# A sliding-window attention with 8 heads inside a three-layer fp32 model step: scores over valid blocks only, the band added by matmul, values divided as they leave PSUM, gates kept in SBUF

## The chip, the core and the metric

One NeuronCore of a Trainium2 chip runs one program. The metric is the device time of one execution in microseconds (us), the median of three runs. TensorE does the matmuls, ScalarE (ACT) and VectorE (DVE) evacuate and transform, GpSimd (POOL) helps, SyncE (SP) starts the weight transfers.

## The reference, cut

The program computes three layers on 512 tokens of width 1024: a first block (a mixer of a gated linear recurrence and a banded attention, a cross-attention to 256 memory tokens, a feed-forward part), and two layers more with five feed-forward parts in all, a latent attention and a gated convolution. The change is in the first block's mixer. Its banded attention has 8 query heads of 64 on 2 key heads; each block of 128 queries sees keys at most 128 away, and each head has a sink in the denominator:

```python
valid = (jnp.abs(qi - kj) <= WINDOW) & (kj >= 0) & (kj < S)
s = jnp.where(valid[None, :, None, None], s, -jnp.inf)
m = jnp.maximum(jnp.max(s, axis=-1, keepdims=True), sk)
p = jnp.exp(s - m)
p = p / (jnp.sum(p, axis=-1, keepdims=True) + jnp.exp(sk - m))
o = jnp.einsum('bnhgqk,bnkhd->bnqhgd', p.astype(v.dtype), vb)
...
merged = jax.nn.sigmoid(gate_r) * y_rec + jax.nn.sigmoid(gate_a) * y_att
return merged @ w_out
```

## The kernel before

Activations lie feature-major: 8 tiles of 128 features x 512 tokens. A weight chunk is 128 x 2048, loaded by SyncE to one of two `stage` slots, and split by ScalarE into a rounded `w_hi` (`split_hi`) and by VectorE into the rest `w_lo` (`split_lo`). A product of two fp32 numbers is three fp32r matmuls (`products`: hi x hi, hi x lo, lo x hi, lines 1744 to 1746); a chunk gives two tiles of 512 tokens, 48 matmuls. Matmuls on plain fp32 operands are recorded as two passes. The order on each engine is the order in which its block of the program is written; semaphores tie the engines. `acc_evac` counts evacuated tiles, `chunk_done` chunks, `lo_ready` split chunks. PSUM has 8 banks of 512 columns; projections rotate through banks 0 to 3.

The stretch of the change comes after the recurrence's twelve chunks ("gla"). First, chunk `kv_a`: tile k feature-major, tile v token-major in 96 matmuls of 128 columns. Then the rotary embedding of k and of four tiles of q: `swap` exchanges feature halves by a matmul with `perm1`, `rotate` on VectorE needs three operations. k stands in `k_pad` with zero blocks at both ends, so that every query block has 384 keys.

Attention runs in tiles j of two heads (p = 0, 1). `scores` (PE) writes 4 blocks x 384 columns to banks 0 to 3, for both heads the same ones; `maxima` (DVE) adds `band` into `w_s` in SBUF, which frees the banks, and takes the maxima; `exponentials` and `divided` (ACT) each pass over `w_s`; `turn` (PE) transposes the ten valid 128 x 128 pieces to banks 4 to 6; ACT rounds them to `wT_hi`, DVE computes `wT_lo`; `values` (PE) makes 12 matmuls into bank 7. A head's `turn` waits for `divided`. The first merge branch is put between the last two heads.

Merge: 8 branches of 24 matmuls, `BRANCHES` alternating the recurrent side (0) and the attention side (1) of output pairs j. Each is multiplied by its gate on DVE. Gate pairs of j = 0, 1 are in `h` (whose residual is read back from DRAM later), those of j = 2, 3 are written to DRAM (`spill`) during gla and read back as `late` and `late_att`. The memory tokens (`mem_raw`) are fetched after the attention; GpSimd sums their squares; a matmul with ones (line 2027) after branch 4 spreads the sum; DVE normalizes four of the eight tiles inside the loop over branches after number 5 and four after it. Then comes the chunk phase `mix_out`.

The same program has a second attention, in the latent layer (8 heads, causal). There the band's counterpart is added by a matmul with the identity, exponentials read PSUM, the transposed probabilities stay fp32, and outputs come token-major, divided on evacuation and transposed back.

## Time and profile before

| | us |
|---|---|
| median of 3 runs | 2855.84 (2854.48 to 2856.95) |
| the profiled execution, its own time | 2857.13 |
| its span, first to last instruction | 2855.3 |
| TensorE busy in the span | 2797.6 (98%) |
| VectorE / ScalarE / GpSimd busy | 1452.4 / 1031.5 / 532.6 |
| stretch from the end of gla to `mix_out` | 298.3 to 457.3 |
| mean granted TensorE clock | 0.990 |

Times in rows are us from the span's start; a row of the timeline has start, duration, engine, line, operation, output<-inputs, partitions x elements, count, and in brackets the idle time before it and what ended that.
### The profile page before, as it was taken

The numbers are of one execution on the slowest core, as the hardware profiler recorded it, in microseconds if no ns is written. First come the engines' busy times: TensorE is split into PE (matmuls) and PEld (weight loads), VectorE is DVE, ScalarE is ACT, GpSimd is POOL, SyncE is SP. The second block draws the span as 40 slices with busy tenths as digits, with TensorE's granted clock in tenths as the row PEclk, the third lists the DMA queues.
The fourth block names the chain that finished last, engine by engine and source line by source line (L and its number), as shares of the span: only waits on it lengthen the run. The fifth ranks groups of instructions, "written<-read, shape, count | busy, mean of one in ns | idle before, by whom it ended". The sixth has DMA issues, their size and how long they took to land.

```text
span 2855.3 us, 33812 instructions
## 1 busy us (share of the span) xinstructions
PE 2797.6 (98%) x12830; PEld 2310.8 (81%) x12830; DVE 1452.4 (51%) x1378; ACT 1031.5 (36%) x1136; POOL 532.6 (19%) x374
## 2 busy tenths in 40 slices
PE   8999888999999999999999999999999999999999
PEld 6978677987888888888868888888888888888887
DVE  5777756547655344443475544334444355644432
ACT  3333553344443234332244343323433222244421
POOL 1124013104001221023230310022100221410100
PEclk9999889999999999999999999999999999999999
DMA  4222113412223332323310222233222332222232
GB/s 161 76 73 96 49 66 104 146 54 103 98 93 103 103 103 88 103 90 106 122 56 31 103 90 101 100 106 103 89 103 88 104 103 102 94 98 95 96 103 88
DMA packets 39818, 270.72 MB, mean 95 GB/s; under 512 B 4416, under 2 KB 4928, under 8 KB 8000
## 3 DMA queue, kind: packets, MB, share of 16 engines
q1 hardware_dynamic: 37152, 259.01, 26.5%
q10 hardware_dynamic: 2592, 10.65, 1.0%
q8 instruction: 55, 0.90, 0.1%
q14 instruction: 19, 0.16, 0.0%
HBM read 265.45 MB, written 4.19 MB: 94 GB/s over the span
## 4 chain that ended last, share of the span: by engine, by line
PE 95%; DVE 2%; ACT 2%; POOL 1%; DMA 1%; issue 1%; ACTq 0%; DVEq 0%; POOLq 0%; SPq 0%
PE ps L1744 30%; PE ps L1746 30%; PE ps L1745 30%; PE ps L1900 1%; PE ps L2248 1%; PE ps L1922 0%; PE ps L2222 0%; PE ps L2146 0%; PE ps L1973 0%; ACT w_s L613 0%; POOL sq L1660 0%; DVE w_lo L898 0%; DMA mem_raw<-in_mem 0%; ACT w_s L622 0%; PE ps L1784 0%
## 5 line engine op out<-in xcount | busy, mean ns | idle before, releaser
L438 ACT ACTIVATE w_hi<-stage 128x2048 fp32r<-128x2048 f32 x241 | 462.1, 1918 | 1378.3 <-PE ps L1746 1376.3
L1744 PE MATMUL ps<-x_hi,w_hi 128*128 128x512 f32 x2392 | 940.7, 393 | 12.4 <-DVE w_lo L973 12.4
L1745 PE MATMUL ps<-x_lo,w_hi 128*128 128x512 f32 x2392 | 931.9, 390 | 0.0
L1746 PE MATMUL ps<-x_hi,w_lo 128*128 128x512 f32 x2392 | 931.8, 390 | 0.0
L898 DVE TENSOR_TENSOR w_lo<-stage,w_hi 128x2048 fp32r<-128x2048 f32 x241 | 605.4, 2512 | 402.0 <-ACT w_hi L438 402.0
L1744 PEld LDWEIGHTS ps<-x_hi,w_hi 128*128 128x128 f32 x2392 | 449.8, 188 | 108.3 <-DVE x_lo L980 12.4
L1745 PEld LDWEIGHTS ps<-x_lo,w_hi 128*128 128x128 f32 x2392 | 449.9, 188 | 95.0 <-issue 3.1
L1746 PEld LDWEIGHTS ps<-x_hi,w_lo 128*128 128x128 f32 x2392 | 449.7, 188 | 94.2
L1744 PE MATMUL ps<-f_hi,w_hi 128*128 128x512 f32 x880 | 342.7, 389 | 0.0
L1745 PE MATMUL ps<-f_lo,w_hi 128*128 128x512 f32 x880 | 342.3, 389 | 0.0
L1746 PE MATMUL ps<-f_hi,w_lo 128*128 128x512 f32 x880 | 342.3, 389 | 0.0
L1614 POOL TENSOR_TENSOR up_b<-up_b,gate_b 128x512 f32<-128x512 f32 x110 | 118.1, 1095 | 1050.9 <-DVE up_b L961 1034.7
L961 DVE TENSOR_TENSOR up_b<-ps,rstd 128x512 f32<-128x512 f32 x110 | 71.0, 687 | 299.2 <-PE ps L1746 299.1
L1745 PEld LDWEIGHTS ps<-f_lo,w_hi 128*128 128x128 f32 x880 | 165.2, 188 | 34.7 <-issue 0.2
L1744 PEld LDWEIGHTS ps<-f_hi,w_hi 128*128 128x128 f32 x880 | 165.2, 188 | 34.6 <-issue 0.2
L1746 PEld LDWEIGHTS ps<-f_hi,w_lo 128*128 128x128 f32 x880 | 165.2, 188 | 34.1
L944 DVE TENSOR_TENSOR gate_b<-ps,rstd 128x512 f32<-128x512 f32 x110 | 71.0, 688 | 230.2 <-PE ps L1746 229.1
L1590 POOL TENSOR_TENSOR sq<-h 128x512 f32 x64 | 78.6, 1228 | 503.6 <-DVE h L923 497.5
L1592 POOL TENSOR_TENSOR ssum<-ssum,sq 128x512 f32<-128x512 f32 x64 | 141.9, 2218 | 5.0
L923 DVE SCALAR_TENSOR_TENSOR h<-ps,h 128x512 f32 (+1 forms) x72 | 46.4, 686 | 141.0 <-PE ps L1746 136.8
L929 DVE SCALAR_TENSOR_TENSOR x_lo<-h,par,x_hi x64 | 104.2, 1666 | 0.0
L485 ACT ACTIVATE f_hi<-up_b 128x512 f32 x110 | 69.6, 633 | 26.9 <-POOL up_b L1614 22.7
(398 smaller groups left out, 2787.6 us busy)
## 6 DMA issues: line engine op xcount, KB each, us to landing
stage<-in_stream SPq DMA_DIRECT2D x242, 1024.0 KB, 4.9
h<-in_x SPq DMA_DIRECT2D x4, 512.0 KB, 7.2
spill<-late ACTq DMA_DIRECT2D x4, 512.0 KB, 2.6
h<-in_x ACTq DMA_DIRECT2D x2, 1024.0 KB, 5.2
out_x<-h SPq DMA_DIRECT2D x8, 256.0 KB, 6.0
stage<-in_stream SPq DMA_DIRECT2D x4, 256.0 KB, 8.1
late<-spill ACTq DMA_DIRECT2D x1, 1024.0 KB, 5.0
late_att<-spill ACTq DMA_DIRECT2D x1, 1024.0 KB, 7.1
```

Of the source, the lines that this page charges most:

```text
L438: act.activation(w_hi[slot][:, :], stage[slot][:, :], ACT.Copy).then_inc(hi_ready, 1)
L485: act.activation(row(f_hi, it * 2 + e), up_b[:, e, :], ACT.Copy).then_inc(f_hi_ready, 1)
L898: dve.tensor_tensor(w_lo[slot][:, :], stage[slot][:, :], w_hi[slot][:, :].bitcast(F32), ALU.subtract).then_inc(lo_ready, 1)
L929: dve.scalar_tensor_tensor(row(x_lo, it * 4 + m), row(h, it * 4 + m), pc(gain, it * 4 + m), row(x_hi, it * 4 + m).bitcast(F32), ALU.mult, ...
L944: dve.tensor_tensor(gate_b[:, e, 1:1 + S], ps[:, (t0 + e) % 4, :], rstd[:, :], ALU.mult).then_inc(acc_evac, 1)
L961: dve.tensor_tensor(up_b[:, e, :], ps[:, (t0 + 2 + e) % 4, :], rstd[:, :], ALU.mult).then_inc(acc_evac, 1)
L1590: pool.tensor_tensor(sq[:, :], row(h, m), row(h, m), ALU.mult).then_inc(sq_ready, 1)
L1592: pool.tensor_tensor(ssum[:, :], ssum[:, :], sq[:, :], ALU.add).then_inc(ss_ready, 1)
L1614: pool.tensor_tensor(up_b[:, e, :], up_b[:, e, :], gate_b[:, e, 1:1 + S], ALU.mult).then_inc(prod_ready, 1)
L1744: pe.matmul(out_ap, wh, xh, start=first, stop=False)
L1745: pe.matmul(out_ap, wh, xl, start=False, stop=False)
L1746: return pe.matmul(out_ap, wl, xh, start=False, stop=last)
```

## The change

Storage and banks. The two heads of a tile get score banks of their own (2, 3, 4 and 0, 1, 5); the turned pieces go back to the same banks. `w_s`, `w_pT` and `mem_raw` take the place of `x_hi` and `x_lo`, which are free once `kv_a` is done. The gates have room in SBUF, `late` and `late_att`, and the DRAM spill is gone.

```diff
+        k_f = place("k_f", TMP, [P, S])
+        k_hi, k_lo = place("k_hi", hid(20), [P, S], F32R), place("k_lo", hid(21), [P, S], F32R)
+        w_s = [place(f"w_s{e}", XH_AT + 3 * e * TILE, [P, 3, S]) for e in range(2)]
+        w_pT = [place(f"w_pT{e}", XH_AT + (6 + 3 * e) * TILE, [P, 3, S]) for e in range(2)]
+        w_o = [place(f"w_o{e}", TMP + (1 + e) * TILE, [P, BLK, P]) for e in range(2)]
...
+        v_f, va = place("v_f", hid(24), [P, S]), place("va", hid(14), [P, BLK, P])
+        wa_const = place("wa_const", hid(12), [P, 4 * P])
+        band, perm1 = wa_const[:, 0:384], wa_const[:, 384:512]
+        wa_const_r = place("wa_const_r", hid(13), [P, 4 * P], F32R)
+        band_r, eye_r = wa_const_r[:, 0:384], wa_const_r[:, 384:512]
...
-        mem_raw = place("mem_raw", hid(16), [P, KT, MEM])
+        mem_raw = place("mem_raw", XH_AT + 12 * TILE, [P, KT, MEM])
...
+        WINDOW_BANKS = [[2, 3, 4], [0, 1, 5]]
+        WINDOW_AT = {1: (0, 0), 2: (1, 0), 0: (2, 0), 3: (2, 2 * P)}
+        WINDOW_OF = TURNED_OF
+        WINDOW_ORDER = [[1], [2], [0, 3]]
+        ROTATED = ["q0", "q1", "q2", "k", "q3"]
+        SWAP_BANK = [5, 6, 7, 5, 6]
```

ScalarE. All gates pass the sigmoid before the last gla chunk's split. Exponentials read PSUM; the division is gone; the third bank's turned piece is a plain copy. `mem_raw` is fetched when `kv_a` is done. Later, the memory's square root and rounding come after all branches.

```diff
-                    spilled_out(3)
+                    act.wait_ge(acc_evac, t + 10)
+                    act.activation(h[:, :, :], h[:, :, :], ACT.Sigmoid).then_inc(gate_sig, 1)
+                    act.activation(late[:, :, :], late[:, :, :], ACT.Sigmoid)
+                    act.activation(late_att[:, :, :], late_att[:, :, :], ACT.Sigmoid).then_inc(gate_sig, 1)
...
-                    act.activation(w_s[p][:, n, :], w_s[p][:, n, :], ACT.Exp, bias=small[:, 4 * p + n:4 * p + n + 1],
-                                   accum_out=small[:, 8 + 4 * p + n:9 + 4 * p + n])
+                    b, c = WINDOW_AT[n]
+                    w = len(WINDOW_OF[n]) * P
+                    act.activation(w_s[p][:, b, c:c + w], ps[:, WINDOW_BANKS[p][b], c:c + w], ACT.Exp,
+                                   bias=small[:, 4 * p + n:4 * p + n + 1], accum_out=small[:, 8 + 4 * p + n:9 + 4 * p + n])
...
-            act.wait_ge(spilled, 64)
-            act.dma_start(late[:, :, :], spill[:, 0:4, :]).then_inc(gates_back, 16)
-            act.dma_start(late_att[:, :, :], spill[:, 4:8, :]).then_inc(gates_back, 16)
+            q_round(1)
+            act.wait_ge(rot_step, 3 * (ROTATED.index("k") + 1))
+            act.activation(k_hi[:, :], k_f[:, :], ACT.Copy).then_inc(k_hi_ready, 1)
+            act.wait_ge(chunk_done, C0["kv_a"] + 1)
             act.dma_start(mem_raw[:, :, :], mem_in).then_inc(mem_landed, 16)
+            exponentials(0)
...
+            exponentials(1)
+            turned(0)
+            q_round(2)
+            for v in range(1, WIN_HEADS):
+                turned(v)
+                if v + 1 < WIN_HEADS:
+                    exponentials(v + 1)
+                if v == 2:
+                    q_round(3)
+                if v == 4:
+                    split_hi((C0["kv_a"] + 2, 0))
+                if v % 2 == 0:
+                    out_hi(v // 2 - 1)
...
-                if j == 2:
-                    act.wait_ge(mem_stat, 1)
-                    act.activation(mem_r, ps[:, 5, 0:MEM], ACT.Sqrt, bias=pc("eps", 0), scale=1.0 / D).then_inc(mem_std, 1)
-                    mem_rounded(0, 4)
...
-            mem_rounded(4, KT)
+            act.wait_ge(mem_stat, 1)
+            act.activation(mem_r, ps[:, 5, 0:MEM], ACT.Sqrt, bias=pc("eps", 0), scale=1.0 / D).then_inc(mem_std, 1)
+            mem_rounded(0, KT)
```

VectorE. Maxima read PSUM per bank. The turned copy replaces the remainder `wT_lo`; `out_divided` multiplies by the reciprocal of the denominator. The rotations of q0 and q1 stand before the evacuation of k. All of the memory's normalization comes after the branches.

```diff
+                for bank, blocks in enumerate(WINDOW_ORDER):
+                    dve.wait_ge(wa_scores, 3 * v + bank + 1)
+                    for n in blocks:
+                        b, c = WINDOW_AT[n]
+                        w = len(WINDOW_OF[n]) * P
+                        ins = dve.tensor_reduce(mx[:, n:n + 1], ps[:, WINDOW_BANKS[p][b], c:c + w], AX.X, ALU.max)
+                ins.then_inc(wa_max, 1)
...
+                dve.tensor_copy(w_pT[p][:, 0:2, 0:384], ps[:, b0:b0 + 2, 0:384]).then_inc(wa_pT, 1)
...
+                dve.tensor_tensor(w_o[j % 2][:, :, half], ps[:, 6, :].rearrange("p (a n) -> p a n", a=BLK)[:, :, half],
+                                  free(small[:, 24 + 4 * p:28 + 4 * p], 0, [[1, BLK], [0, WIN_D]]), ALU.mult).then_inc(wa_ot, 1)
...
+            rotate(0, qa[:, 0, :])
+            rotate(1, qa[:, 1, :])
+            dve.wait_ge(kv_done, 1)
+            dve.scalar_tensor_tensor(k_f[:, :], ps[:, t0 % 4, :], WIN_D ** -0.5, rstd[:, :], ALU.mult, ALU.mult).then_inc(acc_evac, 1)
+            rotate(2, qa[:, 2, :])
+            rotate(3, k_f[:, :])
+            dve.wait_ge(k_hi_ready, 1)
+            dve.tensor_tensor(k_lo[:, :], k_f[:, :], k_hi[:, :].bitcast(F32), ALU.subtract).then_inc(k_ready, 1)
+            rotate(4, qa[:, 3, :])
...
+            maxima(0)
+            maxima(1)
+            for v in range(WIN_HEADS):
+                denominators(v)
+                turned(v)
+                if v:
+                    out_divided(v - 1)
+                if v == 5:
+                    split_lo((C0["kv_a"] + 2, 0))
+                if v and v % 2 == 0:
+                    out_lo(v // 2 - 1)
+                if v + 2 < WIN_HEADS:
+                    maxima(v + 2)
...
-                if i == 5:
-                    dve.wait_ge(mem_std, 1)
-                    dve.reciprocal(mem_r, mem_r).then_inc(mem_std, 1)
-                    dve.wait_ge(mem_std, 2)
-                    mem_normed(0)
-                    for k in range(4):
-                        mem_normed(k + 1)
-                        mem_rest(k)
-            for k in range(4, KT):
```

TensorE. The swaps are spread around the two halves of `kv_a`, and v is made feature-major and transposed by four matmuls. A head's scores take only the valid blocks (256, 384, 384, 256 columns) and add the band by a matmul with `eye_r`. Values are 10 fp32 matmuls of 64 columns. `back` transposes two heads' output. Branch 0 and 1 are spread around the last heads.

```diff
+            def swap(i, src):
+                pe.wait_ge(const_landed, 16)
+                if i >= 3:
+                    pe.wait_ge(rot_step, 3 * (i - 3) + 1)
+                pe.matmul(ps[:, SWAP_BANK[i], :], perm1, src, start=True, stop=True).then_inc(perm_done, 1)
+            def kv_tile(m, done):
+                for k in range(KT):
+                    mm = products(ps[:, (t + m) % 4, :], w_at(c, k * PAIR + m * P, P), (x_hi[:, k, :], x_lo[:, k, :]), k == 0, k == KT - 1)
+                mm.then_inc(done, 1)
+            pe.wait_ge(acc_evac, T0["gla"] + 12)
+            pe.wait_ge(ls_norm, 16)
+            swap(0, qa[:, 0, :])
+            swap(1, qa[:, 1, :])
             begin(c, t, 2)
-            for k in range(KT):
-                products(ps[:, t % 4, :], w_at(c, k * PAIR, P), (x_hi[:, k, :], x_lo[:, k, :]), k == 0, k == KT - 1)
-            for b in range(BLK):
-                for k in range(KT):
-                    mm = products(ps[:, (t + 1) % 4, b * P:(b + 1) * P], (x_hi[:, k, b * P:(b + 1) * P], x_lo[:, k, b * P:(b + 1) * P]),
-                                  w_at(c, k * PAIR + P, P), k == 0, k == KT - 1)
-            mm.then_inc(chunk_done, 1)
-            def swap(i, tile, src):
-                pe.wait_ge(acc_evac, tile + 1)
-                pe.wait_ge(const_landed, 32)
-                if i >= 4:
-                    pe.wait_ge(rot_step, 3 * (i - 4) + 1)
-                pe.matmul(ps[:, 4 + i % 4, :], perm1[:, :], src, start=True, stop=True).then_inc(perm_done, 1)
-            swap(0, T0["kv_a"], k_pad[:, P:P + S])
-            for i in range(WIN_TILES):
-                swap(1 + i, T0["gla"] + 12 * (i // 2) + 10 + i % 2, qa[:, i, :])
-            pe.wait_ge(acc_evac, T0["merge"])
-            pe.wait_ge(k_ready, 1)
-            def scores(j, p, first=False):
+            kv_tile(0, kv_done)
+            pe.wait_ge(acc_evac, t)
+            swap(2, qa[:, 2, :])
+            pe.wait_ge(acc_evac, t + 1)
+            swap(3, k_f[:, :])
+            swap(4, qa[:, 3, :])
+            kv_tile(1, chunk_done)
...
+                for blocks in WINDOW_ORDER:
+                    for n in blocks:
+                        b, at = WINDOW_AT[n]
+                        k0, w = WINDOW_OF[n][0] * P, len(WINDOW_OF[n]) * P
+                        out_ap = ps[:, WINDOW_BANKS[p][b], at:at + w]
+                        products(out_ap, (q_hi[j % 2][half, n * P:(n + 1) * P], q_lo[j % 2][half, n * P:(n + 1) * P]),
+                                 (k_hi[half, k0:k0 + w], k_lo[half, k0:k0 + w]), True, False)
+                        m0 = k0 - (n - 1) * P
+                        mm = pe.matmul(out_ap, eye_r, band_r[:, m0:m0 + w], start=False, stop=True)
+                    mm.then_inc(wa_scores, 1)
...
+                        mm = pe.matmul(ps[:, 6, n * P + WIN_D * p:n * P + WIN_D * (p + 1)], w_pT[p][:, at_bank, at:at + P], va[:, b, half],
+                                       start=(b == WINDOW_OF[n][0]), stop=(b == WINDOW_OF[n][-1]))
...
+            for v in range(WIN_HEADS):
+                turn(v)
+                if v:
+                    values(v - 1)
+                if v == 6:
+                    pe.wait_ge(wa_pT, v + 1)
+                    pe.wait_ge(wa_pT_act, v + 1)
+                    branch(0, range(3))
+                if v and v % 2 == 0:
+                    back(v // 2 - 1)
+                if v + 2 < WIN_HEADS:
+                    scores(v + 2)
+            branch(0, range(3, 4))
+            values(WIN_HEADS - 1)
+            branch(1, range(1))
+            back(3)
+            branch(1, range(1, 4))
...
-                if i == 4:
+                if i == 2:
```

On GpSimd the remainder `q_lo` goes to two buffers; the two memsets of `k_pad` are gone.

The order of instructions shows the moves. TensorE before, from the end of `kv_a` over the swaps (`perm_106`) to the first scores:

```order
L1746 MATMUL ps<-w_hi_54,x_lo 128x128
L1949 MATMUL ps<-k_pad,perm_106 128x512 [waits const_landed,acc_evac]
L1949 MATMUL ps<-qa,perm_106 128x512 [waits const_landed,acc_evac] x3
L1949 MATMUL ps<-qa,perm_106 128x512 [waits rot_step,const_landed,acc_evac]
L1744 MATMUL ps<-k_hi,q_hi 128x384 [waits wa_q,k_ready,acc_evac]
L1745 MATMUL ps<-k_lo,q_hi 128x384
```

TensorE after the change, between the k half (its last matmul first) and the v half of `kv_a` (the permutation is now part of `wa_const`):

```order
L1740 MATMUL ps<-x_hi,w_lo_56 128x512
L1935 MATMUL ps<-qa,wa_const 128x512 [waits const_landed,acc_evac]
L1935 MATMUL ps<-k_f,wa_const 128x512 [waits rot_step,const_landed,acc_evac]
L1935 MATMUL ps<-qa,wa_const 128x512 [waits rot_step,const_landed]
L1738 MATMUL ps<-x_hi,w_hi_54 128x512
L1739 MATMUL ps<-x_lo,w_hi_54 128x512
```

Three swaps moved from behind the chunk to between its halves; two more stand ahead of the k half.

TensorE before, inside the loop over tiles: a head's transposes and the next tile's scores, with their waits:

```order
L1973 MATMUL ps<-const_64,w_s_97 128x128 [waits wa_p]
L1973 MATMUL ps<-const_64,w_s_97 128x128 x9
L1961 REGISTER_ALU [waits wa_q]
L1744 MATMUL ps<-k_hi,q_hi 128x384 [waits wa_s]
L1745 MATMUL ps<-k_lo,q_hi 128x384
```

TensorE after, for head 2: transposes, values of head 1, the transposition back of heads 0 and 1, scores of head 4:

```order
L1991 MATMUL ps<-const_64,w_s_96 128x128 [waits wa_exp]
L1991 MATMUL ps<-const_64,w_s_96 128x128 x9
L2008 MATMUL ps<-va,w_pT_99 128x64 [waits wa_ot,wa_pT_act,wa_pT]
L2008 MATMUL ps<-va,w_pT_99 128x64 x9
L2020 MATMUL ps<-const_64,w_o_100 128x128 [waits va_ready,wa_ot]
L2020 MATMUL ps<-const_64,w_o_100 128x128 x3
L1738 MATMUL ps<-k_hi,q_hi_102 128x384 [waits wa_pT_act,wa_pT,wa_q]
```

The transposes wait for the exponentials and no longer for a division, and the values behind them are those of the head before.

VectorE before, in the merge after branch 5, where the memory's normalization begins:

```order
L898 TENSOR_TENSOR w_lo_57<-stage_53,w_hi_55 128x2048 [waits hi_ready]
L1262 TENSOR_TENSOR late_att<-late_att,late 128x512 [waits acc_evac] x2
L1265 TENSOR_TENSOR mrg_lo<-late_att,mrg_hi 128x512 [waits mrg_hi_ready] x2
L1268 RECIPROCAL rope_c<-rope_c 128x256 [waits mem_std]
L1242 SCALAR_TENSOR_TENSOR rope_s<-mem_raw,par,rope_c 128x256 [waits mem_std]
```

VectorE after, from the evacuation of branch 6 to the same normalization:

```order
L1262 TENSOR_TENSOR late<-late,ps 128x512 [waits gate_sig,branch_done]
L1262 TENSOR_TENSOR late<-late,ps 128x512
L1262 TENSOR_TENSOR late_att<-late_att,ps 128x512 [waits gate_sig,chunk_done]
L1262 TENSOR_TENSOR late_att<-late_att,ps 128x512
L893 TENSOR_TENSOR w_lo_56<-stage_52,w_hi_54 128x2048 [waits hi_ready]
L1267 TENSOR_TENSOR late_att<-late_att,late 128x512 [waits acc_evac] x2
L1270 TENSOR_TENSOR mrg_lo<-late_att,mrg_hi 128x512 [waits mrg_hi_ready] x2
L1272 RECIPROCAL rope_c<-rope_c 128x256 [waits mem_std]
```

The normalization moved behind the evacuations of branches 6 and 7.

## Rows read from the trace of the kernel before

**Rows 1.** The page, chain that ended last, share of the span by engine.
```profile
PE 95%; DVE 2%; ACT 2%; POOL 1%; DMA 1%; issue 1%; ACTq 0%; DVEq 0%; POOLq 0%; SPq 0%
```
**Rows 2.** TensorE's waits, 280 to 480: us in total, times, longest.
```profile
PE ps L1973 <- ACT w_s L622: 9.3, 5, 4.3
...
PE ps L1744 <- issue: 4.2, 1, 4.2
```
**Rows 3.** Busy time by stage; columns: length, PE, PEld, DVE, ACT, POOL, clock, DMA, GB/s.
```profile
298.30:303.50 5.20, 5.20 (x24) 4.30 (x24) 5.17 (x7) 5.10 (x5) 0.00 (x0) 1.00 0.00 0
...
314.40:336.60 22.20, 13.01 (x34) 8.18 (x34) 19.18 (x28) 10.57 (x22) 1.26 (x1) 0.67 0.00 1
336.60:405.20 68.60, 58.10 (x272) 51.05 (x273) 45.84 (x58) 49.06 (x117) 3.80 (x3) 0.78 0.04 16
405.20:457.30 52.10, 40.96 (x172) 33.08 (x171) 33.69 (x41) 20.30 (x20) 16.72 (x16) 0.91 0.46 162
```
**Rows 4.** TensorE's timeline around two waits, then busy time of two stretches.
```profile
354.13 1.31 PE L1973 MATMUL ps<-const,w_s 128*128 128x128 f32 x10 [1.61 <-ACT w_s L622]
356.94 0.68 PE L1744 MATMUL ps<-k_hi,q_hi 64*128 64x384 f32 x1 [1.50 <-POOL q_lo L1651]
...
457.30:461.70 4.40, 4.38 (x10) 3.50 (x11) 4.40 (x5) 0.45 (x1) 0.00 (x0) 0.50 0.02 4
...
356.90:366.60 9.70, 9.66 (x34) 8.90 (x34) 6.23 (x8) 5.17 (x14) 0.00 (x0) 0.50 0.00 0
```
**Rows 5.** TensorE's timeline: two score matmuls, two swaps of q.
```profile
367.44 0.33 PE L1745 MATMUL ps<-k_lo,q_hi 64*128 64x384 f32 x1
367.62 0.33 PE L1746 MATMUL ps<-k_hi,q_lo 64*128 64x384 f32 x1
...
319.54 1.88 PE L1949 MATMUL ps<-qa,perm 128*128 128x512 f32 x4
```
**Rows 6.** The second attention: TensorE's timeline, then busy time of four heads.
```profile
1508.78 1.10 PE L2222 MATMUL ps<-k_h,q_h 128*128 128x512 f32 x2 [1.80 <-ACT l_pT L837]
...
1511.41 1.26 PE L2234 MATMUL ps<-const,l_p 128*128 128x128 f32 x10
1512.51 2.34 PE L2248 MATMUL ps<-v_mla,l_pT 128*128 128x64 f32 x20
1514.69 0.65 PE L2222 MATMUL ps<-k_h,q_h 128*128 128x512 f32 x1
...
1521.25 0.66 PE L2258 MATMUL ps<-const,o_t 128*128 128x128 f32 x4 [0.52 <-DVE o_t L1500]
...
1517.30:1543.10 25.80, 24.73 (x178) 21.28 (x177) 19.31 (x44) 16.44 (x42) 0.00 (x0) 1.00 0.12 42
```
**Rows 7.** Timeline of VectorE and ScalarE; one group of the lines.
```profile
298.48 0.69 DVE L1153 TENSOR_TENSOR TA<-TA,g_silu 128x512 f32<-128x512 f32 x1
...
302.54 1.29 DVE L1160 TENSOR_TENSOR rec_lo<-TA,rec_hi 128x512 fp32r<-128x512 f32 x2
...
1523.18 1.86 DVE L1477 TENSOR_REDUCE small<-ps 128x1 f32<-128x512 f32 x4
...
298.37 1.92 ACT L438 ACTIVATE w_hi<-stage 128x2048 fp32r<-128x2048 f32 x1 [8.94 <-PE ps L1746]
...
301.35 1.28 ACT L596 ACT_TABLE_LOAD   x1
302.64 3.62 ACT L596 ACTIVATE h<-h 128x4096 f32<-128x4096 f32 x1
...
L613 ACT ACTIVATE w_s<-w_s,small 128x384 f32<-128x384 f32 x28 | 16.8, 610 | 0.0
```
**Rows 8.** Timeline of GpSimd, TensorE and VectorE in the merge.
```profile
416.82 0.61 POOL L1657 TENSOR_TENSOR ssum<-mem_raw 128x256 f32<-128x256 f32 x1 [40.83 <-DMA mem_raw<-in_mem]
...
434.17 1.22 PE L2027 MATMUL ps<-ssum,const 128*128 128x256 f32 x2 [6.96 <-POOL ssum L1662]
...
455.94 1.28 DVE L1257 TENSOR_TENSOR late<-late,ps 128x512 f32<-128x512 f32 x2
```

306 lines of the change are left out of this document (126 added, 180 removed).

## The prediction

> **What bounds the kernel now.** I read the chain of work that ended last first: 95% of it is TensorE [rows 1], so a change is worth what it takes out of TensorE's own time line, as work, as a wait or as a slow clock. Then TensorE's waits in the stretch that the change rewrites: 9.3 us for the divided probabilities, 4.2 in front of mix_out [rows 2], and 7.0 for GpSimd's sum of squares [rows 8]. Then the busy time by stage [rows 3]. From the end of the gla chunks (298.3) to the start of mix_out (457.3) it is 159 us: 5.2 for the k half of kv_a, 10.9 for its v half, 22.2 for rotation and first scores (TensorE busy 13.0, granted clock 0.67), 68.6 for the eight heads with the first 24 recurrent matmuls between them (busy 58.1, clock 0.78), 52.1 for the other seven branches (busy 41.0, clock 0.91). A wait here costs twice: after 1.61 us of waiting, ten transposes and 1.50 us more of waiting, the clock fell to the 1.2 GHz level and stayed for 9.7 us of dense work [rows 4].
>
> **Up to the first transposes** (298.3 to 336.6, 38.3 us). Prices at full clock: 24 matmuls of 512 columns 5.4 (the k half has 24 in a window of 5.2, the last one running on [rows 3]), so 0.227 each; a 384-wide one 0.175 from start to start; a swap, which is two passes, 0.9, from four passes in 1.88 [rows 5]. The v half becomes 24 matmuls of 512 columns in place of 96 of 128: 5.4 for the 10.9 between 303.5 and 314.4 [rows 3]. The five swaps stay, but two now run before the k half and three between the halves, so VectorE's rotations (three operations of the kind of which two take 1.29 [rows 7], about 2.1 with their handovers) run beside TensorE and not after it. New order: TensorE, done with gla at 298.3, waits 0.9 for the last norm product, which VectorE finishes at 299.2 [rows 7]; two swaps 1.8; k half 5.4; swap 0.9; wait; two swaps 1.8; v half 5.4. The wait is new: VectorE is busy to 303.8 [rows 7], then does two rotations (4.3) and the evacuation of k (0.7), so k is there at 308.8 and TensorE waits 1.3. That is 17.5, to 315.8. Behind each rotation's wait for its swap only the next rotation and the evacuations are queued on VectorE; the last rotation ends at 316.6, the evacuation of v at 317.3.
>
> Scores of one head: before 12 matmuls of 384. After, only valid blocks: six products of 384 and six of 256, and the band as two of 384 and two of 256; at 0.175, and 0.12 for 256 by proportion, 2.36. So two heads and four transposes of v take 5.2 (to 321.0). The first head's maxima (four reductions, 1.86 [rows 7]) wait for the evacuation of v, end at 319.5, its exponentials (four at 0.61 and a small one, 2.7) at 322.3. TensorE waits 1.3. Total: 24.1 for 38.3, a gain of 14.2. Bounds: 9 (the wait for k doubled, and the clock at half for the swaps as before) to 16 (both waits gone).
>
> **The eight heads** (336.6 to 405.2, 68.6 us). The second attention in this same kernel is already built in the new way, and its rows are the nearest: ten transposes 1.10 (1511.41 to 1512.51), 20 value matmuls of 64 columns 2.18 (1512.51 to 1514.69), four transposes back 0.66 with their drain, so 0.5, after a wait of 0.52; four heads took 25.8 us, 6.45 each, with TensorE busy 24.7 and clock 1.00 [rows 6]. New: 8 x (1.10 + 2.18) = 26.2; six scores 14.2; three transposes back 1.5; the first recurrent branch, 24 x 0.227 = 5.4; together 47.3. Waits: 0.5 before each of the three transposes back, 1.6; one for the first turned copy, which on ScalarE stands behind the copy of v and the second head's exponentials: these end at 325.5, the copy at 326.1, TensorE was free at 323.4, so 2.7 (the like wait in the second attention is 1.80 [rows 6]); and one around the fifth head, where the split of a merge chunk (w_hi, 1.9) goes ahead of an output's rounding on ScalarE, and VectorE's remainder, maxima and next copy queue behind it: 1.2, and 0.3 in front of the branch. Total 53.1 for 68.6, a gain of 15.5. Removed work that was hidden: VectorE's two passes over 1536 columns a head, ScalarE's four divisions. ScalarE needs about 3.7 a head (exponentials 2.7, a turned copy 0.6, its share of roundings) and VectorE 4.1 (maxima 2.1, the copy of 768 columns 1.0, the division 0.4, small ones), both under TensorE's 6.2. Bounds: 6.45 a head and the same branch and first waits give 61, a gain of 8; no fifth-head wait gives 17.
>
> **The merge** (405.2 to 457.3). Seven branches at 5.4 are 38.1 before and after. What goes: the wait of 7.0 for the sums [rows 8], since mem_raw is now fetched at the end of kv_a and GpSimd begins the sums once q_lo of the last tile is done (about 337), 17 us of work from its start at 416.8 to the matmul at 434.2 [rows 8], with some 25 us of room; the slow clock after it, 2.0 (52.1 less 38.1, 7.0, 4.2 and 0.7 for the sums' own matmul, rounded); the wait of 4.2, which is VectorE emptying branch 6 only at 455.94 because the memory's normalization stood ahead of it [rows 8]; and the slow start of mix_out, 10 matmuls in 4.4 us at clock 0.50 [rows 4], 2.1. What comes: a transposition back, 0.5. Gain 14.8. What is late next: the memory's normalization, about 10 us on VectorE, now stands between the merge and the first mix_out evacuation, so the split for mix_out's third chunk ends at about +22.4 us where TensorE wants it at +21.8: 0.7 lost, bounds 0 and 5.
>
> **The gates on chip.** No wait of TensorE names the spill [rows 2], so its removal alone gives nothing. The sigmoids (3.62 for h's 4096 columns, so about 1.9 for each late one's 2048, and a table load of 1.28) move into ScalarE's idle time of 8.94 ahead of the split at 298.37 [rows 7]: 8.7 of 8.94, at nothing; if that cover fell short, the split behind it and the recurrent rounding would be late by the shortfall, under 1 us.
>
> **The clock.** Between the first heads TensorE will wait 1.3, transpose for 1.1, and wait 2.7. Before, 1.61 and 1.50 around the same transposes were followed by 9.7 us at clock 0.50 [rows 4]; in the second attention a wait of 1.80 was not followed by one, since the two passes behind it took 1.10, the full rate [rows 6]. Mine is worse than both, so I count one slow spell of 5 to 10 us, which costs half of itself, as all of it is TensorE's: 3. Bounds 0 and 9 (two such spells).
>
> **The sum.** 14.2 + 15.5 + 14.8 - 0.7 - 3 = 40.8. Against the profiled run's own 2857.1 (span 2855.3 and 1.8 around it) that is 2816.3; that run stands 1.3 above the median of 2855.84, so 2815.0.
>
> **Rivals.**
> (a) No slow spell: waits as costed, clock at 1.00 throughout. 3 us more gain: 2812. For it: the second attention's clock [rows 6]. Against: the slow 9.7 us behind the wait at 356.94 [rows 4]. The Trainium skill, "TensorE: Matmul & The Clock Gate", section "HAM oscillation", ties the fall to one long idle stretch of the engine; none of the waits here is long, so by that rule this rival is the forecast and the time 2812. The trace before the change does not follow it: there the fall came between two short waits.
> (b) The clock falls again and again, as before the change. TensorE keeps waits of 0.5 every other head, and its score matmuls still use 64 rows. Clock 0.78 over the 53 us of the heads would cost 10 to 12 more than (a) has: 2823 to 2828. Against: TensorE's idle time in the heads' stretch falls from 10.5 us to 5.8, most of it at the start. The same page, section "A second HAM failure mode", tells of a clock that goes up and down where the engine idles briefly between groups of matmuls; by it the time would be this rival's, and the stretch before the change at 0.78 agrees.
> (c) The handoffs set the pace: reductions, exponentials, copies and small operations beside GpSimd's sums stretch each head to 8 us and over. 8 x 1.8 = 14 more: 2829 to 2835. Against: the second attention has the same chain at 6.45.
> (d) Slower than before. One mechanism: TensorE's clock stays at the 1.2 GHz level from the first waits at 307 on. Each 1 us of full-rate work then costs 1 us more, so it decides from 44 us of such work on, 88 us of slow running; the stretch to mix_out holds about 100 of it, and slow throughout it would give 2912. For it: the clock was 0.67 and 0.78 over the 90 us from 314.4 to 405.2 [rows 3]. Against: it was 0.91 and not 0.5 in the dense matmuls that follow.
> (e) The change does not do what it says, the waits moving elsewhere with no gain. The order of instructions shows fewer and denser matmuls, and the 7.0 and 4.2 have their causes removed in the order; I give it what "same" has.
>
> **Chances.** Forecast (2813 to 2821) 0.45, (a) and better (2806 to 2813) 0.23, (b) 0.18, (c) 0.09, (d) 0.02, (e) 0.03. The forecast alone is 2815. The range that leaves out two in ten goes from 2807 to 2828. A measurement of this kernel tells about 0.2% (5.7 us) from no change: faster 0.95, same 0.03, slower 0.02.
>
> **What would show it.** In the changed profile: kv_a's v half in about 5.4 us; TensorE waiting about 1.3 for k_f; the second scores ending near 321, the first transposes at about 322; the last value matmuls ending near 375; no wait for GpSimd's sums and none of 4 us before mix_out, which starts near 414; a granted clock of 1.00 but for one spell after 326. It is wrong if a head takes over 7 us with TensorE idle in it (a handoff I placed under cover), if the clock in the heads' stretch is under 0.85, or if mix_out's third chunk waits over 2 us.

## The result, and the profile after

The changed kernel takes 2830.5 us, the median of 20 runs, against 2856.66 for the kernel before, also 20 runs: ratio 0.9925, 95% interval 0.9908 to 0.9942, a gain of 26 us. Forecast were 2815.0 and a range of 2807 to 2828. It is faster, by two thirds of what was forecast. (Of the changed kernel's 28 executions, these and the 8 of section 9, seven took 2841 to 2859 at a mean clock of 0.985 to 0.992, which widens the interval of the ratio without moving the median; of the 26 executions of the kernels with k over 128 rows in sections 2, 4, 8 and 9 none took more than 2815.) The profiled execution has a span of 2827.8, 27.5 shorter than the one before, and its mean granted clock is 0.996.

The chain of work that ended last, by engine, answers to [rows 1]:

```profile
PE 97%; DVE 2%; ACT 1%; DMA 0%; issue 0%; POOL 0%; DVEq 0%; SPq 0%; POOLq 0%; ACTq 0%
```

TensorE's waits between 298 and 480 (us in total, times, longest) answer to [rows 2]. All of them are here:

```profile
PE ps L1738 <- ACT w_pT L628: 1.9, 1, 1.9
PE ps L1935 <- DVE k_f L1219: 1.9, 1, 1.9
PE ps L2020 <- DVE w_o L1207: 1.0, 2, 0.5
PE ps L1935 <- issue: 1.0, 1, 1.0
```

5.8 us in place of 30.9. The 9.3 for the probabilities and the 4.2 in front of mix_out are gone, and so is the 7.0 for the sums. Busy time by stage, with the columns of [rows 3]: kv_a and rotation, scores to the last values, the merge, the first ten weights or so of mix_out:

```profile
298.30:316.00 17.70, 15.03 (x56) 10.49 (x57) 16.60 (x22) 5.32 (x8) 3.06 (x2) 1.00 0.18 60
316.00:393.10 77.10, 74.13 (x413) 60.20 (x411) 34.98 (x79) 28.93 (x88) 12.48 (x17) 0.87 0.08 28
393.10:432.20 39.10, 39.10 (x176) 32.39 (x176) 24.12 (x31) 10.06 (x10) 0.52 (x1) 1.00 0.37 135
432.20:436.60 4.40, 4.40 (x21) 3.65 (x20) 3.47 (x3) 1.92 (x1) 0.00 (x0) 1.00 0.01 2
```

The merge is solid: 39.1 us, all busy, at full clock, and mix_out starts at full clock with 21 matmuls in 4.4 us, where [rows 4] has ten. What is long is the second row: 77.1 us in which TensorE is busy for 74.1. The forecast had 59.6 for it, 7.1 of them waits, and 3 more for a spell of slow clock, which it counted apart. So TensorE is not waiting for a handoff; its own work costs more than I priced it. TensorE's timeline shows which. This is one head's scores at full clock, the first and the third of its four blocks, then the first transposes (start, duration with drain; cost is the distance from start to start):

```profile
340.30 0.44 PE L1738 MATMUL ps<-k_hi,q_hi 64*128 64x384 f32 x1
340.59 0.34 PE L1739 MATMUL ps<-k_lo,q_hi 64*128 64x384 f32 x1
340.76 0.33 PE L1740 MATMUL ps<-k_hi,q_lo 64*128 64x384 f32 x1
341.02 0.44 PE L1979 MATMUL ps<-wa_const_r 128*128 128x384 f32 x1
341.39 0.44 PE L1738 MATMUL ps<-k_hi,q_hi 64*128 64x384 f32 x1
...
342.48 0.38 PE L1738 MATMUL ps<-k_hi,q_hi 64*128 64x256 f32 x1
...
343.34 0.38 PE L1738 MATMUL ps<-k_hi,q_hi 64*128 64x256 f32 x1
...
344.11 1.14 PE L1991 MATMUL ps<-const,w_s 128*128 128x128 f32 x9
```

Between two products the distance is 0.17, the price I used. From the last product to the band matmul (L1979) it is 0.26, from the band matmul to the next product 0.37, and from that product to the second 0.29. A block of 384 columns takes 1.09 (340.30 to 341.39) where 4 x 0.175 = 0.70 was priced, one of 256 takes 0.86 where 0.48 was, a head 3.81 (340.30 to 344.11) where 2.36 was. The shape column tells what changes at just these places: `64*128` for the products, `128*128` for the band matmul. The weight loads (PEld) of the same stretch:

```profile
340.59 0.18 PEld L1740 LDWEIGHTS ps<-k_hi,q_lo 64*128 64x128 f32 x1
341.02 0.19 PEld L1979 LDWEIGHTS ps<-wa_const_r 128*128 128x128 f32 x1 [0.25 <-issue]
341.39 0.18 PEld L1738 LDWEIGHTS ps<-k_hi,q_hi 64*128 64x128 f32 x1 [0.18 <-issue]
341.50 0.19 PEld L1739 LDWEIGHTS ps<-k_lo,q_hi 64*128 64x128 f32 x1
```

A load between matmuls of one row count starts ahead of its matmul, beside the one that runs (340.59 for the matmul at 340.76). Where the row count changes, load and matmul start together (341.02, 341.39), and the loader has sat idle. Every head whose scores ran at full clock throughout takes 3.80 or 3.81, whichever 64 rows its products use.

The clock is the second thing. It is 0.87 in the stretch, with spells at 1.2 GHz from 324.8 to 338.5, from 352.0 to 355.3 and from 369.2 to 372.4. The first begins at the transposes that follow the second head's scores. The other two begin in the last matmuls of a head's scores, here the second:

```profile
352.04 0.31 PE L1740 MATMUL ps<-k_hi,q_lo 64*128 64x256 f32 x1
352.27 0.58 PE L1979 MATMUL ps<-wa_const_r 128*128 128x256 f32 x1
```

A band matmul of 256 columns takes 0.38 at full clock. None of the three has a wait directly ahead of it.

### The profile page after: what moved, and what is told of

Read it like the earlier page. It is cut to its first block, busy times and chain, and to the rows that moved or that the text cites. A ratio compares the mean times of both kernels' runs of the same rounds, so it can differ in the third digit from the quotient of the medians.

```text
span 2827.8 us, 33738 instructions
## 1 busy us (share of the span) xinstructions
PE 2794.9 (99%) x12874; PEld 2304.4 (81%) x12874; DVE 1429.2 (51%) x1387; ACT 1002.0 (35%) x1090; POOL 525.7 (19%) x372
## 4 chain that ended last, share of the span: by engine, by line
PE 97%; DVE 2%; ACT 1%; DMA 0%; issue 0%; POOL 0%; DVEq 0%; SPq 0%; POOLq 0%; ACTq 0%
PE ps L1738 30%; PE ps L1740 30%; PE ps L1739 30%; PE ps L1894 1%; PE ps L2008 1%; PE ps L2287 1%; PE ps L1916 1%; PE ps L2261 0%; PE ps L1979 0%; PE ps L2185 0%; PE ps L1991 0%; DVE w_lo L893 0%; DMA stage<-in_stream 0%; PE ps L1778 0%; DVE KK L1139 0%; PE ps L2273 0%
```

## The experiments

Two questions: what makes a head's scores dear, and what the clock does with them. Then, whether the terms for the merge were right. `products` has other line numbers (1752 to 1754) in kernels with k over 128 rows.

### 1. The band matmul over 64 rows

```
-  mm = pe.matmul(out_ap, eye_r, band_r[:, m0:m0 + w], start=False, stop=True)
+  mm = pe.matmul(out_ap, eye_r[half, :], band_r[half, m0:m0 + w], start=False, stop=True)
```

> The band's matmul is taken over 64 of its 128 rows (the half of the rows that the head's products use), so half of the band is not added; everything else is as in the changed kernel. Its profile shows one head's scores taking 3.81 us at full clock (340.30 to 344.11) where 2.36 was forecast: a block of three products (64 rows) and one band matmul (128 rows) takes 1.09 for 384 columns and 0.86 for 256, and the next weight load stands idle before each change of rows. Theory S (the change between 64-row and 128-row matmuls costs about 0.39 a block): all matmuls of the scores now have 64 rows, a head takes 2.36 to 2.5, eight heads save 10 to 12, time 2819 to 2821, and the low clock spells stay. Rival B (the band matmul is itself dear, through its operand or as fourth in an accumulation): a head stays at 3.8 and the time at 2830. Rival C (what is lost is mainly the clock, and only incidentally the switch): a head's scores get shorter, but the clock's slow spells grow and the time gains under 5.

Measured: 2816.78 (2815.66 to 2824.47), ratio 0.9862 (0.9845 to 0.9878). TensorE's timeline, with product, product, band, product, then the transposes of v behind the head:

```profile
316.58 0.33 PE L1739 MATMUL ps<-k_lo,q_hi 64*128 64x384 f32 x1
316.75 0.34 PE L1740 MATMUL ps<-k_hi,q_lo 64*128 64x384 f32 x1
316.93 0.34 PE L1979 MATMUL ps<-wa_const_r 64*128 64x384 f32 x1
317.11 0.34 PE L1738 MATMUL ps<-k_hi,q_hi 64*128 64x384 f32 x1
...
318.85 0.66 PE L2041 MATMUL ps<-const,v_f 128*128 128x128 f32 x4
```

The same number of matmuls with the same columns, and every distance is 0.17 to 0.18: a head takes 2.55 (316.30 to 318.85), and what it has over 2.36 lies at its edges, where its neighbours have 128 rows. The band matmul is not dear in itself, nor is it dear as the fourth in a sum: rival B has fallen. The gain of 13.7 is above the 10 to 12 of theory S; rival C expected under 5. In the profiled execution (the one at 2824.47) the low clock did not only stay: one spell of 27 us, from 327.8 to 355, takes the place of the three, and the gain there is only 5.2. The other three took 2815.7 to 2817.2. TensorE's clock is the last figure but two:

```profile
324.00:340.00 16.00, 13.91 (x62) 13.60 (x62) 5.54 (x12) 5.28 (x19) 1.28 (x1) 0.62 0.00 1
340.00:375.00 35.00, 33.96 (x213) 32.16 (x212) 18.67 (x43) 15.38 (x45) 11.22 (x16) 0.78 0.02 4
```

Inside a head's scores this kernel has no change of rows, only at their edges, so the low clock does not need the changes inside.

### 2. k over 128 rows

```
-  k_hi, k_lo = place("k_hi", hid(20), [P, S], F32R), place("k_lo", hid(21), [P, S], F32R)
+  k_hi = [place("k_hi0", hid(20), [P, S], F32R), place("k_hi1", hid(22), [P, S], F32R)]
+  k_lo = [place("k_lo0", hid(21), [P, S], F32R), place("k_lo1", hid(25), [P, S], F32R)]
...
-  products(out_ap, (q_hi[j % 2][half, n * P:(n + 1) * P], q_lo[j % 2][half, n * P:(n + 1) * P]),
-           (k_hi[half, k0:k0 + w], k_lo[half, k0:k0 + w]), True, False)
+  products(out_ap, (q_hi[j % 2][:, n * P:(n + 1) * P], q_lo[j % 2][:, n * P:(n + 1) * P]),
+           (k_hi[p][:, k0:k0 + w], k_lo[p][:, k0:k0 + w]), True, False)
```

> The computation is complete. k is kept twice, once with its lower and once with its upper 64 rows zero, so that each product runs over 128 rows with both heads' q as weights; GpSimd writes the four zero halves ahead of its first q_lo, ScalarE and VectorE write each half of k with an instruction of its own (two more instructions, under 1 us, which TensorE's v half covers by about 1). Theory S: all matmuls of the scores have 128 rows, a head takes 2.36 to 2.5 in place of 3.81, 10 to 12 less: 2819 to 2821 if the clock does as in the changed kernel. Theory L (the clock falls because 64-row matmuls make up most of the scores): the spells at 324.8 to 338.5, 352 to 355 and 369.6 to 372.3, which cost some 8 us, go as well: 2811 to 2814, granted clock above 0.98 from 316 to 393. Rival B (band matmul dear): 2830, head 3.8. Rival W (the clock falls because of the waits): scores shorter but the spells after 324.8 stay or grow.

Measured: 2812.25 (2811.81 to 2812.88), ratio 0.9847 (0.9831 to 0.9864), 18 us below the changed kernel; once more on another chip (section 9) 2814.61 beside 2830.10, 15.5 below. One head, from its first product to the transposes of v, and the stage from first scores to last values:

```profile
317.09 0.33 PE L1752 MATMUL ps<-k_hi,q_hi 128*128 128x384 f32 x1
317.26 0.34 PE L1753 MATMUL ps<-k_lo,q_hi 128*128 128x384 f32 x1
317.44 0.34 PE L1754 MATMUL ps<-k_hi,q_lo 128*128 128x384 f32 x1
317.62 0.35 PE L1994 MATMUL ps<-wa_const_r 128*128 128x384 f32 x1
317.80 0.34 PE L1752 MATMUL ps<-k_hi,q_hi 128*128 128x384 f32 x1
...
319.45 0.60 PE L2056 MATMUL ps<-const,v_f 128*128 128x128 f32 x4
...
317.10:376.10 59.00, 55.23 (x410) 53.44 (x409) 33.58 (x77) 29.13 (x88) 12.52 (x17) 0.97 0.11 36
```

317.09 to 319.45 is 2.36, the forecast's price to the hundredth (later heads take some 0.08 more, at the step from the fp32 matmuls ahead of them to their first product, 333.59 to 336.02). The stage takes 59.0 where the forecast had 59.6, and mix_out starts at 415.0 where the forecast's terms give 414.9, both without its slow spell of 3. That they come so close is in part luck: 3.3 less of waiting stands against a slow spell worth 1.7 and small terms. Zeros in half of the rows cost nothing: over 64 rows and over 128 a product of 384 columns takes 0.17 to 0.18 from start to start, so the 64 rows that were left out had been no saving. The clock shows one spell of 3.4 us behind the wait of 2.1 for the first turned copy, one of the same length during the rotations, and 1.00 from 330 on. Theory S holds. For theory L the time is inside its 2811 to 2814, and the stage's clock, expected above 0.98, is 0.97 because of that one spell.

### 3. The band matmuls grouped

```
+  for n in (1, 2, 0):
+      band_of(n, True)
   for blocks in WINDOW_ORDER:
       for n in blocks:
...
-          products(..., True, False)
-          mm = pe.matmul(out_ap, eye_r, band_r[:, m0:m0 + w], start=False, stop=True)
+          mm = products(..., n == 3, n != 3)
+          if n == 3:
+              mm = band_of(n, False)
```

> The computation is complete, and products keep 64 rows. The band matmuls of the first three blocks open their sums ahead of all products, the fourth's closes it behind them (two open sums may not stand in one bank), so a head changes between 128 and 64 rows once forth and once back, where the changed kernel does so four times. Theory S: three of four round trips of 0.39 go, 1.2 a head, 9 in all: 2821 to 2822, a head's scores 2.6 to 2.8. Rival B (the band matmul is dear in itself): a head stays at 3.8, 2830. Rival C (clock): the spells grow, under 5 gained.

Measured: 2821.03 (2819.64 to 2823.39), ratio 0.9881 (0.9864 to 0.9897): 9.5 less than the changed kernel, the expected 9. Here the price of one round trip can be read by itself, since a head has one:

```profile
317.23 0.62 PE L1974 MATMUL ps<-wa_const_r 128*128 128x384 f32 x3
317.78 0.44 PE L1738 MATMUL ps<-k_hi,q_hi 64*128 64x384 f32 x1
318.06 0.33 PE L1739 MATMUL ps<-k_lo,q_hi 64*128 64x384 f32 x1
...
319.73 0.39 PE L1974 MATMUL ps<-wa_const_r 128*128 128x256 f32 x1
319.95 0.60 PE L2048 MATMUL ps<-const,v_f 128*128 128x128 f32 x4
```

The head takes 2.72 (317.23 to 319.95), 0.36 over 2.36. The changed kernel has four round trips and takes 3.81, which is 2.36 + 4 x 0.36. Its blocks taken singly say much the same: 1.09 less 0.70 is 0.39, 0.86 less 0.48 is 0.38. (The head's 3.81 does not hold the first step from 128 rows to 64: it lies ahead of 340.30, and the four transposes of v in front of such a head take 0.53, in the kernel of 2 they take 0.36.) Two kernels, one price, 0.36 to 0.39.

### 4. Both together

```
+  for n in (1, 2, 0):
+      band_of(n, True)
...
+          mm = products(out_ap, (q_hi[j % 2][:, n * P:(n + 1) * P], q_lo[j % 2][:, n * P:(n + 1) * P]),
+                        (k_hi[p][:, k0:k0 + w], k_lo[p][:, k0:k0 + w]), n == 3, n != 3)
```

> The computation is complete: both edits together, k over 128 rows and the band matmuls ahead of the products. Theory S: no change of rows is left to save, so it equals the kernel with k over 128 rows alone within 1 us. Rival B' (part of the price is the band matmul following products into the same sum, not the change of rows): grouping gains again, 3 to 9 us below the kernel with 128 rows alone. It is also the candidate for the best version, with 2811 to 2821 by what the clock does.

Measured: 2813.58 (2811.95 to 2814.82), with k over 128 rows alone 2812.25. That is 1.3 more where 1 was allowed, with overlapping executions; no gain in any case. Grouping gives nothing once the rows are equal, so rival B' has fallen too.

### 5. The kernel before, with scores over 128 rows

```
-  mm = products(ps[:, n, 0:384], (q_hi[half, n * P:(n + 1) * P], q_lo[half, n * P:(n + 1) * P]),
-                (k_hi[half, n * P:n * P + 384], k_lo[half, n * P:n * P + 384]), True, True)
+  mm = products(ps[:, n, 0:384], (q_hi[:, n * P:(n + 1) * P], q_lo[:, n * P:(n + 1) * P]),
+                (k_hi[:, n * P:n * P + 384], k_lo[:, n * P:n * P + 384]), True, True)
```

> The kernel before the change, its scores taken over 128 rows: the sum of two heads' scores in place of one head's, so the output is not the reference's; number and width of matmuls, waits and order are as before. Theory L (64-row matmuls hold the clock down): the clock of 0.67 and 0.78 in the two stretches from 314.4 to 405.2 goes above 0.9, and 8 to 15 us go: 2841 to 2848, the waits staying. Rival W (the clock fell because of the waits for the divided probabilities, 9.3 us): no change of time, 2856, clock as it was.

Measured: 2851.22 (2848.73 to 2853.62) beside 2856.87, ratio 0.9981 (0.9972 to 0.9991): 5.7 less, between the two theories and outside both. The stages that answer to the second and third of [rows 3], and its longest waits:

```profile
314.40:336.60 22.20, 10.79 (x38) 7.48 (x37) 19.10 (x27) 9.81 (x18) 1.38 (x2) 0.84 0.00 1
336.60:405.20 68.60, 53.25 (x294) 46.86 (x293) 46.77 (x61) 49.08 (x117) 3.70 (x3) 0.93 0.09 28
...
PE ps L1973 <- ACT w_s L622: 14.9, 7, 6.1
PE ps L2027 <- DVE late L1257: 7.7, 1, 7.7
```

The clock did rise, from 0.67 to 0.84 and from 0.78 to 0.93, with not one matmul more or fewer. But most of it came back as waiting: for the probabilities 14.9 in place of 9.3, all waits up to 470 together 39.5 in place of 30.9. In the kernel before, the slow clock was in part hidden, because another engine set the pace. In the changed kernel TensorE sets it, and a slow clock is paid in full. The edit does one thing more than its theory says: it also removes the round trip between 128 and 64 rows around each head's scores, which at 0.36 is an estimated 2.9 us at most for eight heads. So the 5.7 is not the clock's alone, and this run does not separate the count of rows from the change of it.

### 6. The memory fetched late again

On the kernel of 2, one part of the change undone.

```
-            act.dma_start(mem_raw[:, :, :], mem_in).then_inc(mem_landed, 16)
             exponentials(0)
...
             out_hi(3)
+            act.dma_start(mem_raw[:, :, :], mem_in).then_inc(mem_landed, 16)
```

> The kernel with k over 128 rows (2812.3), with one part of the change undone: the memory is fetched only when ScalarE has rounded the last window output (about 378), not at the end of kv_a. GpSimd's 17 us of sums then start at about 380.5 and end near 398; the sums' matmul stands at 387.4. Theory of the prediction (part C: the early fetch removed a wait and the slow clock behind it): TensorE waits 10 to 11 for ssum, and 1 to 2 more for the clock: 2823 to 2825. Rival (the sums were covered otherwise, or the wait is made good before mix_out): under 2815.

Measured: 2828.18 (2827.56 to 2828.33), 15.9 above its base, more than the 11 to 13 expected. The wait for the sums, and the clock behind it:

```profile
PE ps L2081 <- POOL ssum L1670: 10.0, 1, 10.0
...
395.00:400.00 5.00, 0.13 (x1) 0.13 (x1) 3.54 (x4) 1.26 (x2) 4.50 (x5) 0.50 0.76 231
400.00:405.00 5.00, 5.00 (x13) 3.90 (x14) 0.00 (x0) 0.00 (x0) 0.53 (x1) 0.53 0.49 188
```

The wait is the 10.0 expected. After it 5 us of solid work ran at 0.53; mix_out starts at 430.0, 15.0 later than at 415.0. What went beyond the expectation is the clock (at 0.53, some 2.4 us of those 5, and a longer spell at 326 to 332) and 1.3 more of waiting for the first exponentials. So the early fetch was worth the most of the merge's parts.

### 7. The memory's normalization ahead again

On the kernel of 2, another part undone. Cut: on ScalarE the square root and the first four roundings go back in front of the last branches' rounding.

```
-            dve.wait_ge(mem_std, 1)
-            dve.reciprocal(mem_r, mem_r).then_inc(mem_std, 1)
...
+                if i == 5:
+                    dve.wait_ge(mem_std, 1)
+                    dve.reciprocal(mem_r, mem_r).then_inc(mem_std, 1)
+                    ...
+                    for k in range(4):
+                        mem_normed(k + 1)
+                        mem_rest(k)
```

> The kernel with k over 128 rows (2812.3), with another part undone: the memory's normalization stands again on VectorE ahead of emptying the seventh branch (and on ScalarE ahead of its rounding), as before the change. Theory of the prediction: the 4.2 us wait for branch 6's bank comes back, and with it mix_out's start at the low clock (2.1); nothing was lost by the late place (0.7 forecast, no wait of mix_out's third chunk seen): 2818 to 2819. Rival 1: the late place costs something elsewhere, so only 2 to 4 come back: 2814 to 2816. Rival 2: with the sums long done the normalization fits ahead of the branch and nothing comes back: 2812.

Measured: 2819.76 (2819.3 to 2820.28), 7.5 above 2812.25 and 5.2 above the base's other measurement of 2814.61. The wait is back to the tenth, and mix_out starts at the low clock:

```profile
PE ps L1758 <- issue: 4.2, 1, 4.2
...
420.00:425.00 5.00, 5.00 (x12) 3.94 (x13) 4.91 (x6) 1.22 (x3) 0.00 (x0) 0.50 0.16 26
```

Both terms of the prediction stand: 4.2 and 2.1 are 6.3, between the 5.2 and the 7.5 measured.

### 8. The first turned copy ahead of the second exponentials

```
-            exponentials(1)
             turned(0)
+            exponentials(1)
             q_round(2)
```

> The kernel with k over 128 rows (2812.3); on ScalarE the first turned copy goes ahead of the second head's exponentials, so that the third scores no longer wait 2.06 for it. Theory (the wait is ScalarE's order): the scores start near 324.9 in place of 326.5; the second transposes wait up to 0.5 for the exponentials, which end about 1.4 later; and the spell of 3.2 us at clock 0.50 behind the wait goes: 2809 to 2811. Rival (the wait moves behind the second transposes and the spell stays): 2812. Above 2813 if the later exponentials hold up the third head too.

Measured: 2810.95 (2810.44 to 2814.27). The wait of 2.1 is now 1.1, for VectorE's part of the copy, and the clock stays at 1.00 behind it:

```profile
325.71 0.41 PE L1752 MATMUL ps<-k_hi,q_hi 128*128 128x384 f32 x1 [1.10 <-DVE w_pT L1203]
```

### 9. On one chip

The changed kernel, the kernels of 2 and 8 once more, and the kernel of 8 with this edit on TensorE (and VectorE's remainder of the output behind the next maxima):

```
-                if v and v % 2 == 0:
-                    back(v // 2 - 1)
                 if v + 2 < WIN_HEADS:
                     scores(v + 2)
+                if v and v % 2 == 0:
+                    back(v // 2 - 1)
```

> The changed kernel itself, to stand on the same chip as the versions beside it: 2830.5 again within 1.5, with its scores at 3.81 a head and its low clock spells. If it comes near 2815 the comparison of the earlier chips misled; theory S and the clock say 17 to 19 above the kernel with k over 128 rows.

> The kernel with k over 128 rows once more, as the base of the two below: 2812 to 2813.

> The first turned copy ahead of the second head's exponentials, once more against its base on one chip: 1.0 to 2.0 faster than the kernel with k over 128 rows, by the wait (2.06 to 1.10) and the low clock behind it. Rival: no difference beyond 0.5, the first measurement (2810.95 against 2812.25) being one of chips.

> The version above, with the transposition back placed behind the next scores in place of ahead of them (on VectorE the remainder of the output behind the next maxima). TensorE waits 0.52 twice for the divided output; the scores need nothing of it and cover it: 1.0 faster than the version above, 2809.5 to 2810.5. Rival: the handoffs to ScalarE and VectorE shift by 2.4 and a wait for the exponentials takes its place: no gain, or up to 1 slower.

| kernel | us |
|---|---|
| before | 2856.84 (2851.37 to 2859.86) |
| changed | 2830.10 (2829.02 to 2859.41) |
| k over 128 rows | 2814.61 (2814.34 to 2814.68) |
| first copy ahead | 2810.67 (2810.19 to 2813.75) |
| and transposition back behind the scores | 2810.70 (2808.99 to 2810.82) |

The changed kernel measures what it did. The first copy's new place gives 3.9 here and gave 1.3 on the other chip, where the base was 2.4 faster; a gain, of a size that is not settled between the two. The transposition behind the scores removes its two waits of 0.5, as all waits that are left show:

```profile
PE ps L1949 <- DVE k_f L1223: 1.9, 1, 1.9
PE ps L1752 <- DVE w_pT L1203: 1.1, 1, 1.1
PE ps L1949 <- issue: 1.0, 1, 1.0
PE ps L2006 <- ACT small L622: 0.7, 1, 0.7
```

and yet the median does not move. In the profiled execution a slow spell stands again behind the wait of 1.1, where the profiles of the same place without this edit show 1.00:

```profile
326.00:328.00 2.00, 2.00 (x8) 2.00 (x7) 0.56 (x1) 2.00 (x8) 0.00 (x0) 0.51 0.04 8
```

It lasts to 329.4 and costs some 1.7, more than the 1 us in question; so the spell that section 8 removed can come back behind the same wait, and 1 us is at the edge of what these runs tell apart. The best versions take 2810.7, ratio 0.9843 (0.9831 to 0.9856) and 0.9840 (0.9828 to 0.9853) to the kernel before, 19 below the changed kernel.

## Why the prediction was wrong

By its own points, with the forecast for each first.

- **Up to the first scores.** 315.8; the first product is at 316.65. The v half came in 5.4 us as 24 matmuls. The wait for k_f was 1.9 for the 1.3 forecast (the forecast's own times, TensorE free at 307.3 and k there at 308.8, make it 1.5).
- **The scores' price: the step that failed.** "At 0.175, and 0.12 for 256 by proportion, 2.36" a head. Measured 3.81: 1.45 x 8 = 11.6 us. The 0.175 of [rows 5] is the distance between two matmuls of 64 rows, and the second attention of [rows 6], from which I took the shape of the new attention, has products and band matmul both of 128 rows: its row at 1508.78 says `128*128`, where the rows at 367.44 and 367.62 say `64x384`. The change puts the one kind between the others eight times a head, and I priced each as if it stood among its like, without a bound for the change of kind. Experiments 1 to 4 settle it: equal rows give 2.36 to 2.55 whichever count it is, one round trip 2.72, four 3.81. The Trainium skill has a rule that I did not draw on: "TensorEngine Tiling (Array Packing)", section "Key Properties", says that a change of the tiling mode drains the engine. That a plain matmul of 64 rows beside one of 128 is such a change is my reading. The trace agrees with it, with a loader that sits idle for 0.18 and 0.25 at the changes shown above, and gives the price here, 0.36 to 0.39 a round trip.
- **The heads' waits.** 7.1 forecast in this stretch, 2.9 measured in the changed kernel. Dearer scores gave the other engines time. In the kernel with the cheap scores they are 3.8, so I had them too high by 3.3 all the same; the wait around the fifth head does not exist.
- **The clock.** One spell, 3 us. In the profile it is three spells, worth 8.2. I read that from TensorE's starts, slow against full: 5.1 from 324.8 to 338.5 (the third head's scores take 6.47 for 3.81, ten transposes 2.13 for 1.09, twice), 1.6 at 352 and 1.5 at 369. Sense and place of the forecast were right (a spell behind the first transposes), the count was not. Rival (b), the clock falling again and again, is nearly half of what happened; it had 10 to 12 for it, which added to (a)'s 2812 makes 2822 to 2824 and not the 2823 to 2828 given. The forecast's sign "clock in the heads' stretch under 0.85" was all but met: it is 0.86 from 322.3 to 393.0.
- **The sum of the heads.** Last values at 375.5 by the terms, 393.1 measured, 17.6 late: 0.9 from the start, 11.6 the scores, 8.2 the clock, 4.2 less of waits, and 1.1 more. Of the 1.1, part is the change of rows in front of a head's scores (0.17 at the transposes of v, section 3), 0.3 is the first branch (5.7 for 5.4), and the rest stays unassigned.
- **The merge.** 39.4 us to mix_out by the terms, 39.1 measured. The early fetch, the late normalization and mix_out's start were forecast right and each was undone on the chip (15.9 and 5 to 7.5 us). For the third chunk 0.7 of waiting was forecast; there was none.
- **The gates.** No wait names them, as forecast. It was not undone by itself.
- **Rival (c)** gave 2829 to 2835, which is where the time fell by luck, for the mechanism is one that did not happen: handoffs that stretch a head to 8 us and over. Heads do take 8.5 us (344.11 to 352.65), but TensorE waits 0.5 in them. The forecast's own sign against itself, "a head takes over 7 us with TensorE idle in it", had the symptom and the wrong cause. A time alone would have confirmed the wrong rival; the timeline refutes it.

With the scores' price alone put right, the forecast's sum gives 2815.0 + 11.6 = 2826.6, inside the range given. Of the other 3.9, 1.8 are in the profiled execution (2829.66 for 2816.3 + 11.6): 5.2 more of slow clock than the 3 forecast and the small terms of 0.9 and 1.1, less 4.2 of waits, 0.3 in the merge and 0.7 for the third chunk, which is 2.0. The last 2.1 are no work at all: the forecast set the median 1.3 below the profiled execution, and it lies 0.8 above. So the price of the scores alone would have left the forecast inside its range; it took the clock as well to bring the time out of it.

## What to carry to other kernels

Before pricing a small matmul between others, compare the shape column of its neighbours: a matmul of 64 rows beside one of 128 is not priced by the distance between two of a kind. If the contraction is 64 and neighbours have 128, padding the streamed operand with a zero half costs no TensorE time and saved 15 to 18 us here, some 12 of them in the scores and the rest by the clock; if padding has no room, group matmuls by row count. And where TensorE is busy all through a stretch that is longer than the sum of its prices, look for the mis-priced instruction before looking for a handoff.

## What the runs showed of the hardware that I had not expected

- **A round trip between 64 and 128 rows costs 0.36 to 0.39 us** at the 2.4 GHz level in fp32r streams (2.72 against 2.36 with one, 3.81 with four). The next weight load does not run beside a matmul of the other row count; it starts with its own matmul, after the loader has sat idle.
- **With the scores over 128 rows the clock held better than over 64.** In the kernel before, 0.67 rose to 0.84 and 0.78 to 0.93 by that edit, which also removed a change of rows at each head. In the changed kernel's family the mean clock of the run was 0.994 to 0.997 (seven executions 0.985 to 0.992) with 64 rows and four changes, 0.996 to 0.997 with one, 0.998 to 0.999 (one execution 0.995) with 64 rows throughout the scores, 0.998 to 1.0 with 128 rows in the kernels of 2, 4, 8 and 9. How much of it is the count of rows and how much the change I did not separate. What tips the clock at 324.8, 352.0 and 369.2 stays open. The nearest waits ahead of the last two are of 0.5 us, up to 348.06 and 365.18, with TensorE busy at full clock from there on; the kernel with k over 128 rows has the same two waits and no spell behind them.
- **A better clock is worth what TensorE's share of the pace is worth.** 5.7 us in the kernel before, where waits grew by 8.6 (and where part of the 5.7 can be the row changes); in the changed kernel, whose waits are 5.8 us in all, each us of slow running costs its half.
